# A new order of the tiles in SBUF: C ahead of XH, and PR between XH and XL

## What is computed

```python
p = h @ w_in                                  # mixer: 1024 -> 6672
merged = sigmoid(gate_dn) * (o_dn @ w_branch_dn) + sigmoid(gate_hg) * (o_hg @ w_branch_hg)
x = x + merged @ w_out
gate, up = split(rmsnorm(x) @ w_up)           # feed-forward: 1024 -> 2 * 2816
x = x + (silu(conv(gate)) * up) @ w_down      # 2816 -> 1024
```

## Time and profile before

| | |
|---|---|
| median of 3 runs | 1721.49 us (1716.86 to 1721.71) |
| the profiled execution | 1721.71 us |
| its span, first to last instruction | 1719.9 us |
| PE busy | 1649.7 us, 96% |
| PE loading weights (PEld) | 1602.2 us, 93% |
| DVE busy | 1229.3 us, 71% |
| ACT busy | 968.1 us, 56% |
| mean DMA rate | 143 GB/s |

### The profile page before, as it was taken

How to read it: one execution, slowest core, us unless ns; L and a number is a source line. 1 busy time by engine, 2 the same in 40 slices (tenths; PEclk the granted TensorE clock), 3 DMA queues, 4 the chain that set the end, 5 groups by cost and what they waited for, 6 DMA issues and landing times.

```text
span 1719.9 us, 30675 instructions
## 1 busy us (share of the span) xinstructions
PE 1649.7 (96%) x13206; PEld 1602.2 (93%) x13206; DVE 1229.3 (71%) x1705; ACT 968.1 (56%) x1426; POOL 7.9 (0%) x14
## 2 busy tenths in 40 slices
PE   6999899999999999899999999999999999899997
PEld 6999899999999899899999998878999998799997
DVE  6889946777747789846777646766688848678863
ACT  6664465565536654555555634347577636567752
POOL 0000000000000000000000000000000000000000
PEclk9999999999999999999999999999999999999999
DMA  6421124465554322125555553520445453055551
GB/s 259 172 74 54 70 74 172 158 210 177 191 182 150 139 72 74 50 74 197 168 191 181 192 177 116 204 95 1 146 173 192 178 195 139 16 196 185 183 195 50
DMA packets 34984, 246.11 MB, mean 143 GB/s; under 512 B 3873, under 2 KB 4257, under 8 KB 5537
## 3 DMA queue, kind: packets, MB, share of 16 engines
q1 hardware_dynamic: 34848, 244.15, 40.2%
HBM read 243.09 MB, written 1.05 MB: 142 GB/s over the span
## 4 chain that ended last, share of the span: by engine, by line
PE 83%; DVE 11%; ACT 5%; issue 1%; DMA 0%; SPq 0%; DVEq 0%; ACTq 0%
PE PS L396 83%; DVE SA L1662 2%; ACT SB L1080 2%; DVE SB L1662 1%; DVE SB L1671 1%; ACT WH L1083 1%; DVE WL L1662 1%; PE PS L399 1%; DVE SB L1902 1%; DVE SA L1827 0%; DVE SB L1906 0%; ACT SB L1609 0%; DVE SB L1666 0%; DVE XL L1671 0%; DVE SA L1671 0%
## 5 line engine op out<-in xcount | busy, mean ns | idle before, releaser
L396 PE MATMUL PS<-XH,WH 128*128 128x256 f32 (+1 forms) x2536 | 727.6, 287 | 23.2 <-DVE WL L1662 21.6
L396 PE MATMUL PS<-XL,WH 128*128 128x256 f32 (+1 forms) x2536 | 719.5, 284 | 0.0
L396 PE MATMUL PS<-XH,WL 128*128 128x256 f32 (+1 forms) x2536 | 719.3, 284 | 0.0
L1083 ACT CAST WH<-RAW 128x2048 fp32r<-128x2048 f32 (+1 forms) x226 | 426.2, 1886 | 437.9 <-PE PS L396 402.0
L1662 DVE TENSOR_TENSOR WL<-RAW,WH 128x2048 fp32r<-128x2048 f32 (+1 forms) x226 | 510.9, 2261 | 156.4 <-ACT WH L1083 152.1
L396 PEld LDWEIGHTS PS<-XH,WH 128*128 128x128 f32 (+1 forms) x2536 | 486.3, 192 | 26.8 <-issue 18.2
L396 PEld LDWEIGHTS PS<-XL,WH 128*128 128x128 f32 (+1 forms) x2536 | 486.3, 192 | 2.6 <-issue 1.9
L396 PEld LDWEIGHTS PS<-XH,WL 128*128 128x128 f32 (+1 forms) x2536 | 486.1, 192 | 0.3
L396 PE MATMUL PS<-INH,WH 128*128 128x256 f32 x960 | 269.5, 281 | 1.1 <-DVE INL L1662 1.1
L396 PE MATMUL PS<-INH,WL 128*128 128x256 f32 x960 | 270.2, 281 | 0.0
L396 PE MATMUL PS<-INL,WH 128*128 128x256 f32 x960 | 267.6, 279 | 0.0
(11 more groups left out here) (139 smaller groups left out, 1556.1 us busy)
## 6 DMA issues: line engine op xcount, KB each, us to landing
RAW<-w_in SPq DMA_DIRECT2D x52, 1024.0 KB, 4.8
RAW<-w_up SPq DMA_DIRECT2D x44, 1024.0 KB, 4.8
RAW<-f_in SPq DMA_DIRECT2D x44, 1024.0 KB, 4.8
RAW<-w_down SPq DMA_DIRECT2D x22, 1024.0 KB, 4.8
RAW<-f_out SPq DMA_DIRECT2D x22, 1024.0 KB, 4.8
RAW<-a_w_in SPq DMA_DIRECT2D x10, 1024.0 KB, 4.8
RAW<-w_out SPq DMA_DIRECT2D x8, 1024.0 KB, 4.8
RAW<-w_bdn SPq DMA_DIRECT2D x4, 1024.0 KB, 4.9
```

The costliest lines, as they stand in the source:

```text
L396: return e.matmul(out, l, r, start=start, stop=stop, skip_group_check=True)
L1083: e.copy(out, x).then_inc(*A.up(*key, of=of))
```

## The change

The order of the declarations changes, nothing else. `C` comes ahead of `XH`, `PR` comes between `XH` and `XL`, `X` follows `XL`. The change is described as one after which `XH` and `XL` begin 8 bytes past a multiple of 16. No instruction, no wait and no transfer is added or removed; `WH`, `WL` and `RAW` lie ahead of the changed stretch.

```diff
         WH, WL = sb("WH", NWS * 2048, R), sb("WL", NWS * 2048, R)
         RAW = sb("RAW", NRAW * 2048)
-        XH, XL = sb("XH", 2048, R), sb("XL", 2048, R)
+        C = sb("C", CN_W)
+        XH = sb("XH", 2048, R)
+        PR = sb("PR", P_W)
+        XL = sb("XL", 2048, R)
         X = sb("X", 2048)
-        C = sb("C", CN_W)
-        PR = sb("PR", P_W)
         MK = sb("MK", 21 * 128, U8)
```

## The result

The changed kernel takes 1701.01 us (median of 4 runs, 1699.70 to 1703.06), against 1719.17 us of the kernel before (4 runs, 1716.60 to 1721.71): a ratio of 0.9892, 95% interval 0.9871 to 0.9913, 18.2 us less. The profiled execution took 1700.58 us, 21.1 less than the profiled one of before. The forecast was 1714.3; the time lies near those of the rival "full move", 1706.9 and 1699.5.

A forecast was written before the change was run, and what follows sets the result against it. The prediction took TensorE (PE) as the bound, through the distance between product starts in the projections. From 1721.71 us it took 7.4 us for XL's step and nothing for the other terms, giving 1714.3 us, range 1700 to 1724.

The forecast's parts named there:

- full move: Rival: XH/XL triples in the projections fall from 360 to 353.3 or 350 ns; 1706.9 or 1699.5 us; chance 0.20.
- partial move: The forecast proper: only XL joins the faster operands, a triple takes 356.7 ns; 1709 to 1718 us; chance 0.42.
- Remainder 8 by 16: Placement of tiles: all begin at multiples of 32, so none has the described remainder, before or after.
- Part 1: XL in XH/XL triples: one of three products gets faster, 360 to 356.7 ns, 2,224 triples on the path, -7.4 us.
- part 2: XH keeps its remainder by 64, costed at nothing; its changed distance to WH bounded by -22.2 and +7.4 us.
- remainder by 64, product by product: Streamed operands at remainder 0 by 64 are slower; each such product in a triple pays 3.33 ns over 350.
- Part 3: narrow: 113.5 ns a step with 16 weight columns, so extra time appears beside a full weight load; its 24 triples nothing.
- Part 4: tokm: 96 triples with XH or XL as loaded operand, 0.3 us either way, taken as 0; steps keep 120 ns.
- Part 5: X, C, PR: ACT on X moves between 620 and 628 ns, 0.3 us at most beside PE's work; counted as nothing.
- Part 7: Other operands' triples, 912 of 1,104 at 353.3: up to 3.0 us less or 0.6 more by execution; only widened the range.
- slower: Rival: XL at another phase than XH costs two steps and saves one; 363.3 ns a triple, +7.4 us, 1729.1; chance 0.11.
- No effect: Rival: XH, streaming twice in a triple, sets the level, or the measure is another; 1721.7 or 1719 us; chance 0.27.

The follow-up runs named there:

- the first experiment: C ahead of XH, PR left behind X, against the kernel before: 1713.01 us (10 runs) against 1720.50, ratio 0.9961.
- The second experiment: PR between XH and XL, C left behind X, against the kernel before: 1708.33 us, one run.

## Why the prediction was right, and where it was wrong

The direction and the place are right: the time fell, by PE's steps in the projections on the path, and nothing took its place as the bound. The size is not: 7.4 us forecast, 18.2 measured. The time lies outside the 1709 to 1718 of the partial move, which was the forecast proper, and within the full range only because that took in the rival "full move", 1 us from its lower end. That it fell within is owed to the rival, and in part to luck: with the level that came true the rival gave 1706.9, and the 6 us below that are other terms.

- **What bounds the kernel** held. PE has no idle time in the projections, the long pieces of the chain shortened by what the steps gave, and even at 340 ns (DMA at 200 GB/s) PE is busy all the time in them.
- **Remainder 8 by 16.** Right that the change does not do this: the tiles start at multiples of 32, and the change works all the same.
- **Part 1, XL's step,** and **part 2, XH at nothing,** are the steps that failed. Both rest on "remainder by 64, product by product". The gap ahead of `WH` shows that the remainder has no part in it. Product by product, the saving should have been 3.3 ns at `XL` and none at `XH`; it was 1.5 ns at `XL` with `WH`, 3.8 at `XH` with `WH` and 1.3 at `XH` with `WL`, although `WH` did not move. The levels are not 350 + 3.33 n either: 351, 352 and 356 came. What my part 2 put at an unseen end, the distance to the weights, is what counts. XH/XL triples went from 360 to 353.3: 2,224 on the path x 6.67 ns = 14.8 us, the smaller of the two gains of the rival "full move". Of its two reasons the distance is shown; the unequal pair has its part as well, since equal pairs at 384 and at 160 did not run at 353.
- **Part 3** pointed the right way, by a reading that does not hold as it stands. In `narrow` not only the width of the load differs from the other projections but the distance too, since its blocks of weights lie 64 bytes apart. Its steps move with the placement as well: 113.5 ns before, 116.1 in the changed kernel, 113.3 with all at distance 192, where a full load also takes 113.3. So the full load alone does not make the extra time. As a hint at distance it deserved more than the 0.20 of a rival.
- **Part 4.** tokm went from 119.8 to 117.8 ns a product, 96 triples x 6 ns = 0.6 us; I had 0.3 at most and forecast that it keeps 120.
- **Part 5** held: ACT and DVE are busy as before, and ACT takes 617 ns over 512 columns of X, 620 before.
- **Part 7** was seen and not used. All 1,104 triples of the other operands ran at 350 in the changed kernel's profile, about 912 of them at 353.3 before: 3.0 us, the size given. They fell in this profile, mostly in the first experiment and partly in the second, but not with the gap ahead of `WH`, nor with `M16` ahead of XH, which both left XH/XL at 360. The second experiment suggests why: within one execution the narrowing projections were at 350 behind XH/XL at 351 and at 353 behind XH/XL at 360. So these 3.0 us seem to be an effect of the change and not of the execution. That the stretch before is the whole reason is not shown: in the first experiment `INH`/`INL` ran at 350 behind 360 as well.

These make 14.8 + 0.6 + 3.0 = 18.4 us, about the 18.2 us between the medians. The granted clock has no need to be in it: runs of the kernel before with a mean clock of 0.988 took 1719.14 and 1719.78 us, and the three of the changed kernel with 0.988 took 1699.70 to 1701.43. The two profiled executions differ by 21.1 us, and their clocks by 0.985 against 0.988. Much of that difference stands in three short pieces. Before, then after (stretch, us, PE busy (x), PE clock, DMA share, GB/s):

```profile
87.16:98.12 10.96, 10.96 (x71) 0.84 0.28 97
596.84:609.05 12.21, 12.21 (x71) 0.75 0.24 87
1126.26:1147.10 20.84, 20.84 (x146) 0.92 0.30 109
```

```profile
87.36:96.55 9.19, 9.19 (x71) 1.00 0.34 116
590.52:601.39 10.87, 10.87 (x71) 0.84 0.30 98
1113.65:1132.71 19.06, 19.06 (x146) 1.00 0.34 121
```

The same products take 44.0 us before and 39.1 after, of which the steps explain at most 0.7 us; granted clocks of 0.84, 0.75 and 0.92 against 1.00, 0.84 and 1.00 mean that before a larger part of these pieces ran at 1.2 GHz. All follow waits of PE for VectorE or ScalarE in the mixers. The first piece of PE in the chain went the other way, 33.09 us before and 33.43 after for 248 products, though its steps alone should have made it 0.5 us shorter. The clock of such pieces can change with the execution alone: the runs of the kernel before, on three chips, had mean clocks from 0.985 to 0.994. Whether the change has any part in it one pair of profiles can't say.

The rival "slower" is out: mixed triples, with XH and XL at different distances, took 351 to 360 ns, none over 360 in an unbroken stretch. "No effect" is out by the interval. The Trainium skill, page "TensorE: Matmul & The Clock Gate" (section "Step-by-step: what each phase is for"), has ports of their own for streaming and loading, so that a load takes no read bandwidth from the running product. By that the place of one operand relative to the other should not matter. The runs differ: with INH/INL moved by 32 bytes (modulo 512) relative to the weights, a triple of theirs went from 350 to 360 ns.

Open: by what mechanism the distance acts, since no view shows accesses to SBUF; whether the distance to `WH` or to `WL` decides (they were the same in all kernels); what picks one of the allowed levels, beyond that it can be handed on; and distances that are no multiple of 32, and 224, which weren't tried. Most placements were run once; their levels are read from one trace each, and a level that did not come may still be allowed.

## What to carry to other kernels

Where TensorE is the bound, divide the distance of two starts by the number of products between them, per operand and per stretch: here differences of 2 to 6% in that distance were worth 1.1% of the kernel (the change) and 2.4% (distance 192), while the durations listed all stayed near 0.28 us. If equal products run at different levels, move the streamed tile by 32 bytes at a time relative to the loaded one, with a gap or by the order of the declarations, and look at the levels; a gap costs 32 bytes of each partition, and the one ahead of `WH` left the time as it was. Move both together once, to tell a distance from an address, and read the starts out of the allocation instead of adding up widths.

## What was not expected of the hardware

- Streaming 256 float32r columns with a 128-column load beside it takes 113.3 to 120.0 ns at the full clock, by the distance of the two operands. For three products, with both halves at one distance: 0 and 96 bytes 360 ns; 32 bytes 350 or 353.3; 64 and 192 bytes 340 or 353.3; 128 bytes 356 or 360; 160 bytes 352, 356 or 360. 256 is as 0, 384 as 128. Unequal pairs have levels of their own: 353.3 for 384 and 160, 351 or 360 for 0 and 288.
- A level, once taken, holds over the whole projection (a thousand products), and at equal distances over the narrowing projection behind it too (seen at 128, 160 and 192 bytes). Another execution of the same program may take another: in the kernel at distance 192 the runs spread over 11 us (1673.18 to 1684.46) at a mean clock of 0.982 to 0.984, where those of the changed kernel spread over 3.4.
